# A fused decoder layer on one core: operand tiles followed chunk by chunk, one transpose group ahead of the last values, and new columns and value stores made later

## The reference

```python
h = rmsnorm(x, norm_mix_g)
q, k, v, a, g = split(h @ w_in)              # 12 heads of 64; a, g: 256 wide
u = a * sigmoid(g)
att = combine(dilated_branch(q, k, v, bias, d, steps) for (128,1), (512,4), (2048,16))
c = silu(layernorm(causal_dwconv31(u)))      # over 256 channels
x = x + concat(att, c) @ w_out
mk, mv = rmsnorm(mem) @ w_k, rmsnorm(mem) @ w_v      # 256 memory tokens
x = x + cross_attend(rmsnorm(x, norm_x_g), mk, mv)   # 4 heads of 256
x = x + (silu(hf @ w_gate) * (hf @ w_up)) @ w_down   # hf = rmsnorm(x, norm_ffn_g), 2816 wide
y = rmsnorm(x, norm_final_g)
```

## Time and profile before

| what | value |
|---|---|
| median of 3 runs | 1938.1 us (1933.88 to 1942.0) |
| the profiled execution's own time | 1934.61 us |
| its span, first to last instruction | 1932.8 us |
| TensorE busy | 1877.0 us, 97% |
| TensorE weight loads busy | 1742.5 us, 90% |
| VectorE busy | 1019.5 us, 53% |
| ScalarE busy | 462.9 us, 24% |
| GpSimd busy | 514.8 us, 27% |
| mean granted TensorE clock | 0.994 of full speed |
| one DMA queue | 219901 packets, 279.94 MB |

### The profile page before, as it was taken

One profiled execution on the slowest core, in us unless ns is written; L12 is line 12 of the kernel. 1 busy time (PEld: TensorE's weight loads), 2 busy tenths in 40 slices (PEclk: granted clock), 3 DMA queues, 4 the chain that ended last, 5 costly groups with the idle time before them and its releaser, 6 DMA issues.

```text
span 1932.8 us, 32913 instructions
## 1 busy us (share of the span) xinstructions
PE 1877.0 (97%) x13193; PEld 1742.5 (90%) x13193; DVE 1019.5 (53%) x2053; ACT 462.9 (24%) x928; POOL 514.8 (27%) x380
## 2 busy tenths in 40 slices
PE   7999998999999999999999999999999999999997
PEld 6999987777777899999659999999999999999997
DVE  6698726666666454612553474544544544544544
ACT  5100013665556521201540130001001001001005
POOL 2332222000000144552002233222222222222234
PEclk9999999999999999999999999999999999999999
DMA  5499967587767512224531142442442442311112
GB/s 157 135 324 338 334 220 222 155 256 226 201 220 239 192 45 77 75 79 160 168 110 33 43 152 86 153 151 87 151 151 87 151 153 85 151 43 43 43 33 93
DMA packets 220001, 281.34 MB, mean 146 GB/s; under 512 B 7521, under 2 KB 206569, under 8 KB 218153
## 3 DMA queue, kind: packets, MB, share of 16 engines
q1 hardware_dynamic: 219901, 279.94, 44.4%
HBM read 266.48 MB, written 113.89 MB: 197 GB/s over the span
## 4 chain that ended last, share of the span: by engine, by line
PE 88%; DVE 5%; SPq 2%; DMA 1%; issue 1%; ACT 1%; POOL 0%; DVEq 0%; POOLq 0%; ACTq 0%
PE bank L1563 26%; PE bank L1597 14%; PE bank L1092 9%; PE bank L1336 8%; PE bank L1353 5%; PE bank L1193 3%; PE bank L1150 3%; PE bank L1039 3%; PE bank L1183 2%; PE bank L1210 2%; PE bank L1316 2%; PE bank L1525 1%; PE bank L1239 1%; PE bank L1164 1%; SPq L657 1%
## 5 line engine op out<-in xcount | busy, mean ns | idle before, releaser
L930 POOL CAST w_hi<-w_raw 128x1024 fp32r<-128x1024 f32 x98 | 106.0, 1082 | 955.7 <-issue 325.6
L1563 PE MATMUL bank<-g_lo,w_hi 128*128 128x362 f32 (+1 forms) x1008 | 334.2, 332 | 0.0
L1563 PE MATMUL bank<-g_hi,w_lo 128*128 128x362 f32 (+1 forms) x1008 | 333.7, 331 | 0.0
L1563 PE MATMUL bank<-g_hi,w_hi 128*128 128x362 f32 (+1 forms) x1008 | 331.1, 328 | 0.0
L932 POOL TENSOR_TENSOR w_lo<-w_raw,w_hi 128x1024 fp32r<-128x1024 f32 x98 | 248.2, 2533 | 7.8
L2612 DVE TENSOR_TENSOR xT<-bank,xT 128x362 f32<-128x362 f32 (+1 forms) x264 | 141.3, 535 | 121.4 <-PE bank L1597 121.4
L1563 PEld LDWEIGHTS bank<-g_hi,w_lo 128*128 128x128 f32 x1008 | 191.3, 190 | 0.0
L1563 PEld LDWEIGHTS bank<-g_hi,w_hi 128*128 128x128 f32 x1008 | 189.8, 188 | 0.2 <-POOL w_lo L932 0.2
L1563 PEld LDWEIGHTS bank<-g_lo,w_hi 128*128 128x128 f32 x1008 | 189.6, 188 | 0.0
L1597 PE MATMUL bank<-act_lo,w_hi 128*128 128x362 f32 (+1 forms) x480 | 157.5, 328 | 0.0
L1597 PE MATMUL bank<-act_hi,w_hi 128*128 128x362 f32 (+1 forms) x480 | 157.5, 328 | 0.0
(11 more groups left out here) (301 smaller groups left out, 3836.3 us busy)
## 6 DMA issues: line engine op xcount, KB each, us to landing
out_sk_dram<-in_cache_win_k_dram SPq DMA_DIRECT2D x24, 2040.0 KB
out_sv_dram<-in_cache_win_v_dram SPq DMA_DIRECT2D x24, 2040.0 KB
kb<-in_cache_win_k_dram SPq DMA_DIRECT2D x48, 512.0 KB, 4.9
vn<-in_cache_win_v_dram SPq DMA_DIRECT2D x22, 1024.0 KB, 7.8
w_raw<-in_w_in_dram SPq DMA_DIRECT2D x22, 512.0 KB, 10.3
w_raw<-in_w_ffn_gate_dram SPq DMA_DIRECT2D x22, 512.0 KB, 3.9
w_raw<-in_w_ffn_up_dram SPq DMA_DIRECT2D x22, 512.0 KB, 3.8
w_raw<-in_w_ffn_down_dram SPq DMA_DIRECT2D x22, 512.0 KB, 3.8
```

Of the source, the lines that this page charges most:

```text
L930: pool.tensor_copy(w_hi[slot][:, :], w_raw[slot][:, :]).then_inc(w_hi_done, 1)
L1563: last = pe.matmul(out, w, r, start=start, stop=stop)
```

## The change

Seven edits, of which none adds or removes arithmetic:

- **a.** Token tile 2 is split directly behind tiles 0 and 1, ahead of the scaling of tile 3. The first two weight tiles wait for the first half of the chunks of their last token tile at matmul 0, and for the second half at matmul 12.
- **b.** `store_v(c)` for c = 0 to 3 is issued one weight load later.
- **c.** `new_rows` stands behind `read_values` and the last two `turned_keys` of its step.
- **d.** After the last step, `turn_sample_p` stands ahead of `values` on TensorE, its softmax ahead of `turned_p` on ScalarE, and the `FILL` numbers follow. The wait for the last values read moves from chunk 0 to chunk 5 of `attended_hi(0)`.
- **e.** O tile 0, Q tile 0 and the first gate tile wait for the rest part of one chunk at a time (`split` in `project`), not for all eight of a group.
- **f.** The first two tiles of the cross attention's output projection are taken out of the loop. Token group 0 of the first waits for 14 of 16 `xv_lo`, group 1 for 16, and group 2 for the sample results.
- **g.** Line numbers behind the edits move by up to 18.

```diff
-            return {0: [], 1: [], 2: [0, 1], QT: [QT - 1, QT]}.get(t, [t - 1])
+            return {0: [], 1: [], 2: [0, 1, 2], 3: [], QT: [QT - 1, QT]}.get(t, [t - 1])
...
         number("P", STEPS - 1, 5)
+        number("PS", UNITS - 1, 3)
         number("O", STEPS - 1, 1)
-        number("PS", UNITS - 1, 3)
...
-                if n >= FIRST_QKV + 5 and which < 2:
-                    (store_k, store_v)[which](c)
+                if n >= FIRST_QKV + 5 and which != 1:
+                    (store_k, None, store_v)[which](c)
...
-                if n < 2:
-                    t0, w = GROUPS[g]
-                    pe.wait_ge(lo_done, 2 * ((t0 + w - 1) // P + 1))
...
+                    for m in range(8 * third, 8 * third + 8):
+                        if n < 2 and m in (0, 12):
+                            pe.wait_ge(lo_done, 2 * ((sum(GROUPS[g]) - 1) // P) + 1 + m // 12)
+                        _, out, w, r, start, stop = products[m]
...
             turn_p(STEPS - 1)
+            turn_sample_p(UNITS - 1)
             values(STEPS - 1)
-            turn_sample_p(UNITS - 1)
...
+                            if j == 0 and m % 3 == 0:
+                                pe.wait_ge(split, KC * g + m // 3 + 1)
...
+            for j in range(2):
+                slot, use = weight_turn(N_XO + j)
+                pe.wait_ge(w_ready[slot], use)
+                for g in range(3):
+                    if j == 0 and g == 0:
+                        pe.wait_ge(xv_lo, 14)
+                    elif j == 0 and g == 1:
+                        pe.wait_ge(xv_lo, 16)
+                    elif j == 0:
+                        for n in range(6, 8):
+                            xread("W", n)
+                    pe.wait_ge(r_added, 30 + 3 * j + g + 1)
...
-                    pe.wait_ge(fn_lo, KC * (g + 1))
...
+                            if k == 0 and m % 3 == 0:
+                                pe.wait_ge(fn_lo, KC * g + m // 3 + 1)
...
+            sample_softmax(UNITS - 1)
             turned_p(STEPS - 1)
-            sample_softmax(UNITS - 1)
...
+                    if g == 0 and k == PAIRS - 1:
+                        f = FILL["O", STEPS - 1, 0]
+                        act.wait_ge(t_free[f % 3], f // 3 + 1)
...
-                if d % 8 == 0:
-                    new_rows(d // 8)
                 if d:
                     read_values(d - 1)
                 if not second:
                     turned_keys(u, 1, [2, 3])
+                if d % 8 == 0:
+                    new_rows(d // 8)
...
+            inverse_sample_sum(UNITS - 1)
             read_values(STEPS - 1)
-            inverse_sample_sum(UNITS - 1)
```

More of the change, by code:

```diff
@@ L1037, in _ @@
                 for third in range(3):
-                    for _, out, w, r, start, stop in products[8 * third:8 * third + 8]:
+                    for m in range(8 * third, 8 * third + 8):
+                        if n < 2 and m in (0, 12):
+                            pe.wait_ge(lo_done, 2 * ((sum(GROUPS[g]) - 1) // P) + 1 + m // 12)
+                        _, out, w, r, start, stop = products[m]
                         last = pe.matmul(out, w, r, start=start, stop=stop)
@@ L1325, in turn_mem, with project @@
                 last.then_inc(m_kv_turned, 1)
-            def project(kind, j, ready, free, beside_it):
+            def project(kind, j, ready, free, beside_it, split=None):
                 slot, use = m_place(kind, j)
@@ L1383, in free @@
                 def free(g):
-                    if j == 0:
-                        pe.wait_ge(cv_lo, KC * (g + 1))
-                    elif j == 1:
+                    if j == 1:
                         pe.wait_ge(t_free[g % 3], FILLS[g % 3])
-                    else:
+                    elif j:
                         pe.wait_ge(r_added, 3 * j + g + 1)
@@ L1403, in beside_it @@
                             turn_mem(m)
-                project("O", j, r_ready, free, beside_it)
+                project("O", j, r_ready, free, beside_it, cv_lo)
             def project_q(j):
                 def free(g):
-                    if j == 0:
-                        pe.wait_ge(n_lo, KC * (g + 1))
-                    elif j == 1:
+                    if j == 1:
                         pe.wait_ge(n_rms, 3)
-                    else:
+                    elif j:
                         pe.wait_ge(xq_done, 3 * (j - 2) + g + 1)
@@ L1421, in beside_it @@
                         norm_spread(tools_x, 0, bank[3:6])
-                project("Q", j, xq_ready, free, beside_it)
+                project("Q", j, xq_ready, free, beside_it, n_lo)
             pe.wait_ge(sc_free, 6 * STEPS)
@@ L1539, in _ @@
                         turn_c_out(n)
-            pe.wait_ge(xv_lo, 16)
-            for n in range(6, 8):
-                xread("W", n)
-            project_stream(N_XO, KC // 2, None, (g_hi, g_lo), residual_banks, GROUPS,
-                           r_added, r_ready, 6, 30)
+            for j in range(2):
[10 more added lines that the diff above has]
+                    pe.wait_ge(r_added, 30 + 3 * j + g + 1)
+                    for _, out, w, r, start, stop in proj_products(slot, g_hi, g_lo, GROUPS[g:g + 1],
+                                                                   residual_banks[j][g:g + 1]):
+                        last = pe.matmul(out, w, r, start=start, stop=stop)
+                    last.then_inc(*((r_ready, 1) if g < 2 else (w_used[slot], 1)))
+            project_stream(N_XO + 2, KC // 2 - 1, None, (g_hi, g_lo), residual_banks, GROUPS,
+                           r_added, r_ready, 6, 36)
             ffn_prods = [[proj_products(s, g_hi, g_lo, GROUPS, bank[3 * s:3 * s + 3]) for s in range(2)]]
@@ L1577, in first_gate_up @@
                             pe.wait_ge(n_rms, 6)
-                        for _, out, w, r, start, stop in ffn_prods[0][k][3 * KC * g:3 * KC * (g + 1)]:
+                        for m, (_, out, w, r, start, stop) in enumerate(ffn_prods[0][k][3 * KC * g:3 * KC * (g + 1)]):
+                            if k == 0 and m % 3 == 0:
+                                pe.wait_ge(fn_lo, KC * g + m // 3 + 1)
                             last = pe.matmul(out, w, r, start=start, stop=stop)
@@ L1779, in _ @@
             act.wait_ge(v_out, 96)
-            f = FILL["O", STEPS - 1, 0]
-            act.wait_ge(t_free[f % 3], f // 3 + 1)
             attended_hi(0)
```

## The result

The changed kernel takes 1921.3 us in the median of six runs (1918.4 to 1927.3), the kernel before beside it 1939.9 us. The ratio is 0.9907, 95% interval 0.9892 to 0.9921. The profiled execution took 1918.4 us with a span of 1916.6 us, where 1919.0 and 1917.2 had been forecast, and the median 1920.5. The median fell by 18.6 us and the span of the profiled execution by 16.2, where 15.6 had been forecast. The forecast of the total held. Its terms held less well, and they are what there is to learn from.

The account below looks back on a forecast made before the run. TensorE bounds the kernel, busy 1877.0 of 1932.8 us. Terms 2.0 + 0 + 9.4 + 2.0 + 1.3 + 0.9 = 15.6 us give 1919.0 us, or 1922.5 from the median; predicted 1920.5, range 1914 to 1929 us.

Parts of the forecast that it names:

- a: Start: first group begins at 15.65 us, then tile 3 is late; gain 2.0 us, 1.4 if the clock falls.
- b: Value stores, stage 2: what tile 17 saves is waited for at tile 19, so 0 us.
- c: New columns in attention steps 0, 8 and 16: pauses go and some clock returns; 9.4 us, ends 7.3 and 11.
- d and e: End of attention and O tile 0: starts some 3.2 us earlier, only 2.0 us stay; ends 2.0 and 4.5.
- Q tile 0: TensorE's wait for the third group there goes, as its first parts are ready: 1.3 us.
- f: Cross attention's output projection: start still held by the step of r_added, so 0.9 us and not 1.7.
- the upper end of 4.5 us or more: Value stores, best case: the whole wait for tile 19 and the slow clock behind it go, 4.5 us gained.
- The slack: Attention: the moved copies end before the next scores arrive, with 0.7 us to spare in step 8, 0.4 in step 0.
- The clock not won back: Rival for start and attention: half clock stays, gain 12.8 us, or 11 if another stretch slows; 1923 to 1925 us; chance 0.22.
- Copies on the scores' path: Rival in attention: copies end after the scores arrive, up to 8.4 us come back, gain 7.2, 1929 us; chance 0.12.
- Slower through the stores: Rival in stage 2: four moved stores add 23.6 us of issue time, a loss of 8.0, 1944 us; chance 0.03.
- Edit f as it says: Rival at the cross attention's output: 1.7 us gained, 1919.7 us, or a later gate gives 0; no separate chance.

Follow-up runs that it names:

- run 5: Changed kernel without the value stores of pairs 0 to 3 (those rows of out_pv not written): 1914.3 us, ratio 0.9855 to the kernel before.
- run 9: Changed kernel with the last read_sample and the step of r_added each ahead of the last two rest parts on VectorE: 1924.5 us, ratio 0.9913.
- run 7: Changed kernel with each of the sixteen copies of new_rows made as two of half the width, 32 in all: 1931.5 us, ratio 0.9943.
- run 11/12: Changed kernel with edit d undone, then with edit e undone; end-of-attention stretch 14.15 and 13.19 us (12.34 with both edits); no total time given.
- run 8: Changed kernel with the transposes of token tiles 3 to 6 one to two thirds of a group later: 1921.8 us, ratio 0.9909.
- Run 4: The changed kernel once more, unaltered, on the chip of the three kernels behind it: 1925.7 us, ratio 0.9928 to the kernel before.

## Why the prediction was right, step by step

- **The total.** Forecast 15.6, found 16.2 in the spans. The terms were off by -2.6 (a), +2.2 (b), +1.95 (c), +0.6 (d, e), +0.5 (Q tile 0), -0.1 (f), -0.4 (feed-forward) and -1.6 (the end), which sum to +0.6. They cancelled, and that the sum came within 0.6 us is luck. On another chip the same kernel stands at 0.9928, which is 14 us.
- **a, mis-sized: 2.0 forecast, 0.35 found.** The step that failed is "the scaling runs from 17.3 to 19.2 us at its 1.91 us". It took 2.93. The second part of it is the clock: I priced it at 0.9 us, for 3 us of work, and behind the longer pause it stayed at half for 5.1 us of work, 2.5 us. Before, the scaling ran beside a cast of GpSimd (to 16.58 us) and then beside its subtraction:

```profile
16.66 3.22 POOL L932 TENSOR_TENSOR w_lo<-w_raw,w_hi 128x1024 fp32r<-128x1024 f32 x1
```

After, it ran beside the subtraction from 17.23 to 19.08. It takes 1.28 us where GpSimd is idle. In two other profiles (runs 5 and 9) it began some 0.35 us earlier beside the same subtraction (16.91 and 16.86), took 3.24 and 3.31 us, and ended no earlier. So its end follows that of the subtraction. The Trainium skill, GPSIMD Engine Reference, 1. Specifications, says that GpSimd and VectorE share their path to SBUF and contend where a VectorE instruction has two SBUF inputs; this one has two. The trace agrees. No run moves the subtraction by itself, so this cause is argued and not shown.
- **b, right: 0.** The mechanism (tile 17's gain is waited for at tile 19) is what the times of the weights show: 3.0 us earlier for tile 17, the same for tile 19 within the spread. The 2.2 us of the first profile did not repeat: 245.1 us in the second, 245.7 without the edit. What the sum didn't look at is what the stores cost wherever they stand: without them the stretch is 4.5 to 9 us shorter (run 5), as much as the upper end of 4.5 us or more.
- **c, right mechanism, mis-sized: 9.4 forecast, 11.35 found.** The pauses went as forecast. The failed term is the clock: I counted the transposes directly behind the pauses of steps 0 and 16, 1.1 us each, and found 1.4 and 1.7. Another 1.7 us lay behind a later wait of step 0, which I had not looked at. Why that wait is followed by half clock before and not after, no run takes apart; in run 7, where TensorE idles more ahead of it, it is again. The wait for the next sample keys took 0.7 back (0.4 to 1.1 us), which the sum did not have. Pauses 7.3, clock 4.8 and keys -0.7 make the 11.4 found. The slack was right to 0.2 us, and run 7 shows that it is real.
- **d and e, right: 2.0 forecast, 2.6 found.** The second group gave back 1.0 us (1.2 forecast) and the first started 3.6 earlier (3.2).
- **Q tile 0, 1.3 forecast, 1.8 found;** run 11/12 puts 1.6 of it on edit e. **f, 0.9 forecast, 0.83 found,** and the cause, the place of the step of `r_added`, is shown by run 9.
- **The rivals.** The clock not won back: false for attention, true for the start and for the end of the kernel. Copies on the scores' path: not here, but 1.1 us more copying brings it. Slower through the stores: no. Edit f as it says (1.7 us) or worth 0: neither. Whether the longer half clock in the last transposes (1.6 us) comes from the change stays open. It lasts 3.4 us before and with edit c alone, but also in two kernels with nearly all edits (runs 5 and 8), and 6.8 us in the other ten profiles, so the change at least does not force it.

## What to carry to other kernels

Price a pause of the matrix engine by the length of the half-clock stretch in the clock's rows, not by the few instructions directly behind it, and look for a second stretch behind the next wait. When a step is moved, take its duration from a row with the same neighbour on the engine that it shares memory with. Before costing the order of transfers in a full queue, ask what their absence would give, and compare stage lengths in several profiles of the same code: the stage that waits for transfers differed by 4.5 us here, the attention stage by 0.6 at most where the pause described next is absent.

## What the runs showed of the hardware

**A pause with no releaser.** In five of the fourteen profiles TensorE stops in step 15 behind the tenth of 36 values, for 3.3 to 4.2 us. Timeline without edit b, then the transfers of 524 to 530 us there:

```profile
524.73 0.82 PE L1211 MATMUL bank<-p_T,v_nat 128*64 128x128 f32 x10
...
528.83 1.74 PE L1211 MATMUL bank<-p_T,v_nat 128*64 128x128 f32 x26 [3.29 <-issue]
```

```profile
q1 hardware_dynamic: 1206, 1.92, 105.0%
q8 instruction: 1, 0.02, 1.2%
```

One packet of the instruction queue lies in the pause, at 526.3 us, beside sample loads that fill the DMA engines (share 1.05 here). It hits the same instruction each time, and the stage is 3.6 to 5.5 us longer in four of them (the fifth is run 7, with its own excess). The packets of that queue part the two groups. In the nine profiles without the pause, one starts 6.1 to 6.4 us ahead of the tenth value. In the five with it, none starts in the 14 us ahead of it; one starts 1.0 to 2.0 us behind it, and TensorE resumes 2.5 to 2.6 us after that. So it looks like code that came late. What delays the packet stays open, as no run tried it.

**A granted clock of 1.00 over slow matmuls.** In the run with later transposes the matmuls 0.30 us apart lie under this row:

```profile
16.00:19.00 3.00, 3.00 (x10) 3.00 (x11) 2.29 (x3) 2.41 (x6) 2.92 (x2) 1.00 1.05 363
```

The Trainium skill, TensorE: Matmul & The Clock Gate, Seeing it yourself, warns that such clock events have been unreliable. The trace agrees: at the start, the spacing of equal matmuls told more than the clock's column. Run 4 has the same spacing there.
